# Splitting the narrow last slabs by their own columns, spreading the block sums, and moving the merge sigmoids

## The chip, the cores and the metric

One NeuronCore of a Trainium2 chip runs the whole program. The engines are TensorE (PE; its weight loads are listed as PEld), VectorE (DVE), ScalarE (ACT), GpSimd (POOL) and SyncE (SP), which issues most of the transfers. Time is the device time of one execution in microseconds (us), the median of the runs shown.

## The reference

256 tokens of width 2048 pass through two layers of a first block and one layer of a second block, all in fp32. Cut to what the change touches:

```python
# first block, twice: the input projection, of which the fourth group (rwkv) has 1792 columns
u = rms_norm(h, norm_pre_mix[l])
p = u @ w_in[l]
p_ret, p_hgrn, p_ml, p_rw = split_cols(p, GROUP_COLS)    # 512*3 + 64 + 64 + 128 = 1792 in p_rw
...
# second block: qa, kc, vc, ks, vs, kw, vw and ga are 1024 + 6*256 + 48 columns
proj = h @ w_in
(qa, kc, vc, ks, vs, kw, vw, ga, za, qb, kb, vb, zb, ma, mb) = jnp.split(proj, IN_SPLITS, axis=-1)
...
def compress(t, pe, w1, w2):        # of kc and of vc
    blk = t[:, cidx] + pe[None, None, :, None, :]
    blk = blk.transpose(0, 1, 3, 2, 4).reshape(B, n_c, G, CMP_BLOCK * dh)
    return jax.nn.gelu(blk @ w1) @ w2
...
merged = jax.nn.sigmoid(ma) * ya + jax.nn.sigmoid(mb) * yb     # ma and mb: 2048 columns each
```

## The kernel before

**Products.** Activations lie feature-major: 128 features on the partitions, 256 tokens along the free dimension. A weight is brought in as slabs of four 128-row tiles by 512 columns (1 MB) into a ring of four. Each fp32 product is made from parts: ACT writes a rounded high part of the slab (`high`, L185, tile `w_hi`), DVE subtracts it from the slab to get the low part (`low`, L193, tile `w_lo`), and PE multiplies the high weights with the high and low activations side by side (L214, 512 columns) and the low weights with the high activations (L215, 256 columns). `w_hi` and `w_lo` have two places each. So the high part of slab g+2 waits until PE has used slab g, the low part waits for the high part, and PE waits for the low part.

**A projection.** `Linear` runs over chunks of 512 columns; with an inner size of 2048 a chunk is four slabs. Columns that don't fill a chunk make a last, narrow one: 256 columns in the rwkv projection of each layer (12 full and 4 narrow slabs), 128 columns in the qkv projection of the second block (20 full and 4 narrow slabs). The transfer of a narrow slab brings only its columns, and PE multiplies only those; `high` and `low` run over all 2048 elements of the place (`self.slot`).

**The order on ACT and DVE** comes from `ahead`: for every slab g first the part of slab g+2, then a callback `beside`, and at the last slab of a chunk the epilogue. ACT's epilogue copies the cross sums out of PSUM (L343), waits for DVE's sum (L364, or L366 into `tmp`), and applies a function (L348) if there is one. Most chunks run in a hardware loop of 8 slabs; the last ones of a stage are written out. When the narrow chunk ends, both engines have also split slab 0 of the next stage (`split_next`); the stage ends when all engines are done.

**The block sums.** In the qkv projection `beside` is `Blocks`: DVE adds the position weights to 4 groups of the compressed-key rows, four additions a group (L2871), behind the low parts of slabs 18, 19, 20 and 21, one group each. Before the first group DVE waits for the transfers that gather those rows.

**The merge projection.** `mixes` is the 4096 columns of `ma` and `mb`: 8 chunks of 4 slabs with a sigmoid. On PE all 8 chunks run in a loop of two chunks; on ACT and DVE the first six run in that loop, and the last two are written out. The seven first chunks' sigmoids are in place; the eighth is done in the next stage (`defer`).

Of the kernel before, what the change touches and what calls it, by code (L numbers as in the profile page):

```python
# [6 lines left out]
F32 = mybir.dt.float32  # L7
F32R = mybir.dt.float32r
I32 = mybir.dt.int32
ALU = mybir.AluOpType  # L10
ACT = mybir.ActivationFunctionType
AX = mybir.AxisListType

P = 128
T = 256
D = 2048
# [7 lines left out]
CW = 512  # L24
CB = CW // P
SK = 4
RING = 4
# [6 lines left out]
class Signal:  # L34


    def __init__(self, ctx, nc, name):
        self.sem = ctx.enter_context(nc.semaphore(name))
        self.base = 0
        self.seen = 0  # L40
# [80 lines left out]
class Stream:  # L121
# [56 lines left out]
    def high(self, act, g, i=None):  # L178

        core = self.core  # L180
        if g >= 2:
            self.reached(act, core.slab_used, g - 2, i)
        self.landed(act, g, i)
        at = slice(0, self.slot)
        core.nc.scalar.activation(core.w_hi[:, g % 2, at], core.ring[:, (self.start + g) % RING, at], ACT.Copy)\  # L185
            .then_inc(core.hi_ready, 1)

    def low(self, eng, g, i=None, ops=None):

        core = self.core  # L190
        self.reached(eng, core.hi_ready, g, i)
        at = slice(0, self.slot)
        (ops or core.nc.vector).tensor_tensor(core.w_lo[:, g % 2, at], core.ring[:, (self.start + g) % RING, at],  # L193
                                              core.w_hi[:, g % 2, at].bitcast(F32), ALU.subtract).then_inc(core.lo_ready, 1)

    def used(self, eng, g, i=None):

# [32 lines left out]
class Linear(Stream):  # L230
# [6 lines left out]
    def __init__(self, core, mats, k, col0, cols, dst, kind="copy", func=ACT.Copy, src=None, x0=0, tail=None, row0=0, unrolled=False):  # L237
        self.x0, self.tail, self.row0 = x0, tail, row0
        self.mats, self.dst, self.kind, self.func, self.src_tiles = mats, dst, kind, func, src
        self.kt = k // P  # L240
        self.slabs = self.kt // SK
        self.body = BODY // self.slabs
        self.col0 = col0
        self.m = len(mats)
        full, self.last = divmod(cols, CW)
        self.n_chunks = full * self.m
        assert not (self.m == 2 and self.last)
        self.trips = 0 if unrolled else self.n_chunks // self.body
        self.total = self.n_chunks + (1 if self.last else 0)

        self.ahead_trips = self.trips if self.trips * BODY + 2 <= self.total * self.slabs else self.trips - 1
        super().__init__(core, self.total * self.slabs, BODY)

    def width(self, q):
        return CW if q < self.n_chunks else self.last

    def ends(self, dst, g, i):
        q, s = divmod(g, self.slabs)
        row = self.row0 + s * SK * P
        rows = self.mats[q % self.m][row:row + SK * P, :].rearrange("(k p) n -> p k n", p=P)  # L260
        col = self.col0 + q // self.m * CW
        n = self.width(q)
        dst = dst.rearrange("p (k n) -> p k n", k=SK)[:, :, 0:n]
        if i is None:
            return dst, rows[:, :, col:col + n]
        return dst, rows[:, :, bass.ds(i * (self.body // self.m * CW) + col, n)]

    def ahead(self, eng, part, epilogue, after):

        split = dict(high=self.high, low=self.low)[part]  # L270
        for g in range(self.split, 2):
            split(eng, g)

        assert self.post is None or self.ahead_trips <= 0

        def step(g, i):
            if g + 2 < self.n_slabs:
                split(eng, g + 2, i)
            elif g == self.n_slabs - 2:
                self.split_next(eng, part, after)  # L280
            if self.beside is not None and i is None:
                self.beside(eng, part, self.n_slabs - 1 - g)
            if g % self.slabs == self.slabs - 1:
                q = g // self.slabs
                if self.post is not None and part == "low" and q >= 2:
                    self.post.fold(eng, q - 2)
                if not (self.defer and q == self.total - 1):
                    epilogue(eng, q, i)
                if self.post is not None and part == "high" and q:
                    _, turn, _ = self.where(q - 1, i)  # L290
                    free = self.core.free[(q - 1) % 2]
                    eng.wait_ge(free.sem, free.base + turn + 2)
                    self.post.early_square(eng, q - 1)
                    if q < 3:
                        self.post.scale(eng, q - 1, q)
                    else:
                        last = self.core.free[q % 2]
                        eng.wait_ge(last.sem, last.base + turn + 2)
                        self.post.early_square(eng, q)
                        self.post.load_root(eng)  # L300
            if self.early is not None and i is None:
                self.early(eng, part, self.n_slabs - 1 - g)

        if self.ahead_trips > 0:
            with eng.Fori(0, self.ahead_trips) as i:
                if part == "high" and self.kind == "gate":
                    self.core.nc.scalar.activation(self.core.table[:, :], self.core.const("ones")[:, 0:1], ACT.Silu)
                for g in range(BODY):
                    step(g, i)
        for g in range(max(self.ahead_trips, 0) * BODY, self.n_slabs):  # L310
            step(g, None)
# [17 lines left out]
        eng.wait_ge(free.sem, self.base[free] + q // 2 + 2 + opened)  # L329

    def act_epilogue(self, act, q, i):
        core, nc = self.core, self.core.nc
        par, turn, at = self.where(q, i)
        n = self.width(q) // P
        free, tmp = core.free[par], core.tmp[:, par, 0:n, :]
        trip = 0 if i is None else i * self.body
        self.used(act, (q + 1) * self.slabs - 1, i)

        act.wait_ge(free.sem, self.base[free] + turn + 1)
        if self.kind == "gate" and par == 0:  # L340

            act.wait_ge(core.free[1].sem, self.base[core.free[1]] + turn + 1)
        nc.scalar.activation(tmp, core.ps[:, CB * par:CB * par + n, T:2 * T], ACT.Copy).then_inc(core.cross_copied.sem, 1)  # L343
        if self.plain() or self.kind in ("times", "plus") or (self.kind == "gate" and par == 1):
            return
        act.wait_ge(core.summed.sem, self.base[core.summed] + q + 1 + trip)
        if self.kind == "copy":
            nc.scalar.activation(self.out_tiles(q, at, n), tmp, self.func).then_inc(free.sem, 1)  # L348
        elif self.kind == "mul":
            nc.scalar.activation(tmp, tmp, self.func).then_inc(core.factor_ready.sem, 1)  # L350
        else:
            nc.scalar.activation(tmp, tmp, ACT.Silu).then_inc(free.sem, 1)
# [125 lines left out]
class Idle:  # L478
# [5 lines left out]
    act = pool = sp = pe  # L484
# [233 lines left out]
class Down(Stream):  # L718
# [46 lines left out]
    def __call__(self, eng, part, left):  # L765

        x_split = self.x_high if part == "high" else self.x_low
        if left == 3:
            x_split(eng, 0)
            x_split(eng, 1)  # L770
        elif left == 2:
            x_split(eng, 2)
# [479 lines left out]
class Lead:  # L1252
# [49 lines left out]
    def act(self, act, stream, first_split):  # L1302
# [55 lines left out]
        for q in range(4):  # L1358
            high(q)

    def dve(self, dve, stream, first_split):
# [63 lines left out]
        if first_split == 0:  # L1425
            stream.low(dve, 0)
        norm(1)
        low(0)
        norm(2)
        low(1)  # L1430
# [1394 lines left out]

class Blocks:

    def __init__(self, m, w, qkv):  # L2830
        self.m, self.w, self.qkv = m, w, qkv
# [26 lines left out]

    def __call__(self, eng, part, left):

        if part == "high" or not 4 <= left < 8:
            return
        if left == 7:
            eng.wait_ge(self.moved.rec[0], 16 * 4)
            eng.wait_ge(self.weights.rec[0], 16 * 5)
        g = 7 - left
        for n in range(2):
            view = self.m.arena[:, 52 + 4 * n + g, :].rearrange("p (c b two) -> p b c two", b=8, two=2)
            for half in range(2):
                rows = slice(half * 8, half * 8 + 8)  # L2870
                self.m.nc.vector.tensor_tensor(self.blk[n][:, rows, g * NCMP:(g + 1) * NCMP], view[:, :, half:half + NCMP, 0],  # L2871
                                               self.pe_v[n][:, rows].unsqueeze(2).broadcast_to([P, 8, NCMP]), ALU.add)
# [372 lines left out]
def second_block(m, a, qkv, lead, out_stored, result):  # L3245
# [4 lines left out]
    w_in = a["w_in_2"][0]  # L3250
    ada = m.second("ada")

    def proj(c0, n, dst, kind="copy", func=ACT.Copy, src=None, tail=None):
        return Linear(m, [w_in], D, c0, n, dst, kind, func, src, tail=tail)

    stored, reloaded, fetched = Load(m, "stream_stored"), Load(m, "stream_reloaded"), Load(m, "compress_weights_landed")
    tiles, there, spare = Tiles(m.a(0, N_ARENA)), Tiles(m.h[:, :, :]), Tiles(m.spare[:, :, :])
# [33 lines left out]
    for j in range(8):  # L3291
        g = j // 2
# [10 lines left out]
    add = [masks[:, tt * T:(tt + 1) * T] for tt in range(2)]  # L3303
# [143 lines left out]
```

## Time and profile before

| | us |
|---|---|
| median of 3 runs | 3932.89 |
| lowest and highest | 3929.29, 3940.15 |
| span of the profiled execution | 3928.8 |
| PE busy in it | 3659.1 (93%) |
| DVE, ACT, POOL busy | 2039.1, 1771.8, 1717.0 |

The profiled execution's own time is listed only as its span, which is 0.5 us under the lowest run and 4.1 us under the median. In the timelines below the first number is the start in us from the span's start, the second the duration of the merged group; the bracket at a row's end is how long the engine had been idle and what released it.

### The profile page before, as it was taken

The page shows a single profiled execution, that of the slowest core. Times are in us where ns is not written, and L with a number is a line of the kernel's source. Part 1 is how long each engine was busy: PE and PEld are TensorE (multiplying, and loading weights), DVE is VectorE, ACT ScalarE, POOL GpSimd, SP SyncE. Part 2 cuts the span into 40 slices and gives each one's busy share as a digit, 9 for nine tenths or more (in the row PEclk, how much of TensorE's full clock was granted, in tenths as well). Part 3 has the DMA queues.
Part 4 walks back from the last instruction along what each step waited for, and adds up shares of the span by engine and source line. Part 5 has one row for each costly group of instructions (what it writes and reads, how often), then busy time and mean ns, then how long its engine had stood idle before and what let it go on. Part 6 is the DMA issues. An engine that isn't in the chain of part 4 may idle for free. (4 is left out here: it accounts for less than half of the span.)

```text
span 3928.8 us, 60889 instructions
## 1 busy us (share of the span) xinstructions
PE 3659.1 (93%) x25724; PEld 3246.5 (83%) x25724; DVE 2039.1 (52%) x2013; ACT 1771.8 (45%) x1865; POOL 1717.0 (44%) x824
## 2 busy tenths in 40 slices
PE   8898899899999999798999799999999999989998
PEld 7788888688888887687889688888887788878887
DVE  4747533655555555646542555555556542244474
ACT  4415444544444445415444544444445334544443
POOL 0426566499991000424656399994000045440000
PEclk9999899999999999998999999999999999999999
DMA  5423345477775554423435477775554633426553
GB/s 190 140 66 124 110 139 192 158 240 238 241 241 187 192 182 138 141 67 104 130 118 170 154 246 235 241 241 198 183 186 160 207 105 114 124 89 203 182 174 126
DMA packets 378828, 655.47 MB, mean 167 GB/s; under 512 B 13713, under 2 KB 189921, under 8 KB 377745
## 3 DMA queue, kind: packets, MB, share of 16 engines
q1 hardware_dynamic: 363248, 596.98, 46.8%
q0 software_dynamic: 15392, 55.79, 4.2%
q8 instruction: 142, 2.33, 0.2%
q14 instruction: 46, 0.37, 0.0%
HBM read 645.37 MB, written 6.29 MB: 166 GB/s over the span
## 5 line engine op out<-in xcount | busy, mean ns | idle before, releaser
L214 PE MATMUL ps<-x_parts,w_hi 128*128 128x512 f32 x6160 | 2184.0, 399 | 68.2 <-DVE w_lo L193 25.7
L215 PE MATMUL ps<-x_parts,w_lo 128*128 128x256 f32 x6160 | 1730.8, 281 | 0.0
L193 DVE TENSOR_TENSOR w_lo<-weight_ring,w_hi 128x2048 fp32r<-128x2048 f32 x392 | 957.5, 2443 | 1034.6 <-ACT w_hi L185 1034.4
L214 PEld LDWEIGHTS ps<-x_parts,w_hi 128*128 128x128 f32 x6160 | 1163.8, 189 | 362.3 <-issue 36.9
L185 ACT ACTIVATE w_hi<-weight_ring 128x2048 fp32r<-128x2048 f32 (+1 forms) x412 | 787.9, 1912 | 1153.2 <-PE ps L215 1085.1
L215 PEld LDWEIGHTS ps<-x_parts,w_lo 128*128 128x128 f32 x6160 | 1169.7, 190 | 0.0
L627 PE MATMUL ps<-x_parts,w_hi 128*128 128x256 f32 x2592 | 782.8, 302 | 69.4 <-ACT arena L645 33.7
L628 PE MATMUL ps<-x_parts,w_hi 128*128 128x256 f32 x2592 | 748.0, 289 | 0.0
L629 PE MATMUL ps<-x_parts,w_lo 128*128 128x256 f32 x2592 | 747.0, 288 | 0.0
L627 PEld LDWEIGHTS ps<-x_parts,w_hi 128*128 128x128 f32 x2592 | 512.2, 198 | 101.6 <-issue 58.6
L578 POOL TENSOR_TENSOR w_lo<-weight_ring,w_hi 128x1024 fp32r<-128x1024 f32 (+1 forms) x152 | 376.8, 2479 | 345.9 <-ACT w_hi L575 338.6
L628 PEld LDWEIGHTS ps<-x_parts,w_hi 128*128 128x128 f32 x2592 | 512.9, 198 | 4.5 <-issue 3.6
L629 PEld LDWEIGHTS ps<-x_parts,w_lo 128*128 128x128 f32 x2592 | 511.9, 198 | 0.0
L590 POOL TENSOR_TENSOR w_lo<-weight_ring,w_hi 128x1024 fp32r<-128x1024 f32 (+1 forms) x152 | 354.2, 2330 | 277.3 <-ACT w_hi L587 262.3
L2809 POOL TENSOR_SCALAR spare<-spare,second_vectors 128x512 f32<-128x512 f32 x180 | 406.3, 2264 | 3.9
L2813 POOL TENSOR_TENSOR arena<-arena,spare 128x512 f32<-128x512 f32 x180 | 356.4, 1980 | 14.6
L193 POOL TENSOR_TENSOR w_lo<-weight_ring,w_hi 128x2048 fp32r<-128x2048 f32 (+1 forms) x20 | 91.5, 4577 | 596.3 <-ACT w_hi L185 596.3
L575 ACT ACTIVATE w_hi<-weight_ring 128x1024 fp32r<-128x1024 f32 (+1 forms) x152 | 154.3, 1015 | 276.8 <-PE ps L629 276.8
L587 ACT ACTIVATE w_hi<-weight_ring 128x1024 fp32r<-128x1024 f32 (+1 forms) x152 | 154.3, 1015 | 209.2 <-PE ps L629 196.7
L115 POOL DMA_DIRECT2D spare<-in_w_ada x96 | 73.5, 765 | 150.2 <-POOLq L391 70.8
L115 POOL DMA_DIRECT2D arena<-in_w_ck x4 | 3.3, 826 | 295.2 <-DVE w_lo L193 295.2
L3184 DVE SCALAR_TENSOR_TENSOR arena<-ps,arena 128x256 f32<-128x256 f32 (+1 forms) x40 | 20.4, 553 | 163.8 <-PE ps L3090 129.8
(407 smaller groups left out, 2835.0 us busy)
## 6 DMA issues: line engine op xcount, KB each, us to landing
weight_ring<-in_w_in SPq DMA_DIRECT2D x212, 1024.0 KB, 5.2
weight_ring<-in_w_ffn_gate SPq DMA_DIRECT2D x88, 1024.0 KB, 5.2
weight_ring<-in_w_ffn_up SPq DMA_DIRECT2D x88, 1024.0 KB, 5.2
weight_ring<-in_w_ffn_down SPq DMA_DIRECT2D x88, 1024.0 KB, 5.2
spare<-in_w_ada POOLq DMA_DIRECT2D x96, 512.0 KB, 5.0
weight_ring<-in_w_out SPq DMA_DIRECT2D x32, 768.0 KB, 4.7
weight_ring<-in_w_out SPq DMA_DIRECT2D x24, 1024.0 KB, 5.1
weight_ring<-in_w_br_a SPq DMA_DIRECT2D x8, 1024.0 KB, 5.2
```

Source lines behind the costliest of these rows:

```text
L185: core.nc.scalar.activation(core.w_hi[:, g % 2, at], core.ring[:, (self.start + g) % RING, at], ACT.Copy)\
L193: (ops or core.nc.vector).tensor_tensor(core.w_lo[:, g % 2, at], core.ring[:, (self.start + g) % RING, at], core.w_hi[:, g % 2, at].bitcas ...
L214: mm(out, hi, core.x_parts[:, x, :, :].rearrange("p a t -> p (a t)"), start=first, stop=False)
L215: return mm(out[:, 0:T], lo, core.x_hi[:, x, :], start=False, stop=last)
L575: core.nc.scalar.activation(hi, src, ACT.Copy).then_inc(core.upper_high.sem, 1)
L578: core.nc.gpsimd.tensor_tensor(lo, src, hi.bitcast(F32), ALU.subtract).then_inc(core.upper_low.sem, 1)
L590: core.nc.gpsimd.tensor_tensor(lo, src, hi.bitcast(F32), ALU.subtract).then_inc(core.lo_ready, 1)
L627: mm(out, hi, x_hi, start=(kk == 0), stop=False)
L628: mm(out, hi, x_lo, start=False, stop=False)
L629: last = mm(out, lo, x_hi, start=False, stop=(kk == 2 * self.ks - 1))
L2809: ins = nc.gpsimd.tensor_scalar(to, buf[:, n % 2, k, :], c[:, 2 * s + k:2 * s + k + 1], None, ALU.mult)
L2813: done(pool, nc.gpsimd.tensor_tensor(out, out, buf[:, n % 2, k, :], ALU.add), step)
```

## The change

- `high` and `low` go through a new `filled`: in the narrow slabs they touch only the columns that were loaded (four pieces of 256 or 128 elements), in the others the whole place as before.
- `Blocks` has a table `GROUPS_AT`: group 0 behind the low part of slab 19, groups 1 and 2 behind that of slab 20, group 3 behind that of slab 21.
- `proj`, which builds only the merge projection, sets `unrolled=True`: its chunks are written out on PE, ACT and DVE. With a function and a plain copy it is also `late`: ACT copies the cross sums at the chunk's last slab, and applies the sigmoid one step later, behind the next high part.

```diff
 def high(self, act, g, i=None):
...
-        at = slice(0, self.slot)
-        core.nc.scalar.activation(core.w_hi[:, g % 2, at], core.ring[:, (self.start + g) % RING, at], ACT.Copy)\
+        core.nc.scalar.activation(self.filled(core.w_hi[:, g % 2, :], g), self.filled(core.ring[:, (self.start + g) % RING, :], g), ACT.Copy)\
...
+        lo, src, hi = (self.filled(x, g) for x in (core.w_lo[:, g % 2, :], core.ring[:, (self.start + g) % RING, :], core.w_hi[:, g % 2, :]))
+        (ops or core.nc.vector).tensor_tensor(lo, src, hi.bitcast(F32), ALU.subtract).then_inc(core.lo_ready, 1)
...
+    def filled(self, slab, g):
+
+        n = self.width(g // self.slabs)
+        return slab if n == CW else slab.rearrange("p (k n) -> p k n", k=SK)[:, :, 0:n]
...
+        self.late = unrolled and kind == "copy" and func != ACT.Copy
...
+            if self.late and part == "high" and g % self.slabs == 0 and g:
+                self.act_function(eng, g // self.slabs - 1, None)
...
-                if not (self.defer and q == self.total - 1):
+                if self.late and part == "high" and q < self.total - 1:
+                    self.act_cross(eng, q, None)
+                elif not (self.defer and q == self.total - 1):
                     epilogue(eng, q, i)
...
+    GROUPS_AT = {6: (0,), 5: (1, 2), 4: (3,)}
...
-        return Linear(m, [w_in], D, c0, n, dst, kind, func, src, tail=tail)
+        return Linear(m, [w_in], D, c0, n, dst, kind, func, src, tail=tail, unrolled=True)
```

`act_cross` and `act_function` are the two halves of the former `act_epilogue`, which now calls both.

On DVE, at the end of the qkv projection, from the low part of slab 18 to the stage's end (`w_lo` is a low part, L2871 and L2898 are the block sums, L364 and L387 the chunk sums), before:

```order
L193 TENSOR_TENSOR w_lo<-weight_ring,w_hi 128x2048
L2871 TENSOR_TENSOR arena<-arena 128x8x15 x2
L2871 TENSOR_TENSOR spare<-arena 128x8x15 x2
L193 TENSOR_TENSOR w_lo<-weight_ring,w_hi 128x2048
L2871 TENSOR_TENSOR arena<-arena 128x8x15 x2
L2871 TENSOR_TENSOR spare<-arena 128x8x15 x2
...
L364 TENSOR_TENSOR arena<-ps,tmp 128x1024
L193 TENSOR_TENSOR w_lo<-weight_ring,w_hi 128x2048 x3
L364 TENSOR_TENSOR tmp<-ps,tmp 128x256
```

and of the changed kernel:

```order
L192 TENSOR_TENSOR w_lo<-weight_ring,w_hi 128x2048 x2
L2898 TENSOR_TENSOR arena<-arena 128x8x15 x2
L2898 TENSOR_TENSOR spare<-arena 128x8x15 x2
L192 TENSOR_TENSOR w_lo<-weight_ring,w_hi 128x4x128
...
L192 TENSOR_TENSOR w_lo<-weight_ring,w_hi 128x4x128
L2898 TENSOR_TENSOR arena<-arena 128x8x15 x2
L2898 TENSOR_TENSOR spare<-arena 128x8x15 x2
L387 TENSOR_TENSOR arena<-ps,tmp 128x1024
L192 TENSOR_TENSOR w_lo<-weight_ring,w_hi 128x4x128 x2
L192 TENSOR_TENSOR w_lo<-weight_ring,w_hi 128x2048
L387 TENSOR_TENSOR tmp<-ps,tmp 128x256
```

The two full low parts (slabs 18 and 19) now stand together ahead of the first group, and the low parts of slabs 20 to 23 have a quarter of the elements; the last low part, of the next stage's slab 0, is a full one in both.

On ACT, in the merge projection, one turn of the loop before (`w_hi` is a high part, L343 and L359 the cross copy, L348 and L371 the sigmoid):

```order
L185 ACT_TABLE_LOAD
L185 ACTIVATE w_hi<-weight_ring 128x2048
...
L343 ACTIVATE tmp<-ps 128x1024
L346 ISA
L348 ISA
L348 ACT_TABLE_LOAD
L348 ACTIVATE arena<-tmp 128x1024
...
L343 ACTIVATE tmp<-ps 128x1024
L346 REGISTER_ALU
L348 ISA
L348 ACTIVATE arena<-tmp 128x1024
```

and the first three chunks of the changed kernel:

```order
L184 ACTIVATE w_hi<-weight_ring 128x2048 x5
L359 ACTIVATE tmp<-ps 128x1024
L184 ACTIVATE w_hi<-weight_ring 128x2048
L371 ACT_TABLE_LOAD
L371 ACTIVATE arena<-tmp 128x1024
L184 ACTIVATE w_hi<-weight_ring 128x2048 x3
L359 ACTIVATE tmp<-ps 128x1024
L184 ACTIVATE w_hi<-weight_ring 128x2048
L371 ACTIVATE arena<-tmp 128x1024
```

One high part now stands between each cross copy and its sigmoid, and of two table loads a turn one is left in the whole stage. In the rwkv projections only the shapes change (128x4x256 in place of 128x2048 for slabs 12 to 15), not the order; POOL's and SP's rows are the same in both kernels.

## Rows read from the trace of the kernel before

**Rows 1.** The page, part 1: busy time and share of each engine.

```profile
PE 3659.1 (93%) x25724; PEld 3246.5 (83%) x25724; DVE 2039.1 (52%) x2013; ACT 1771.8 (45%) x1865; POOL 1717.0 (44%) x824
```

**Rows 2.** PE's waits in 75:112, 1500:1660, 2990:3180, 3530:3740: total, times, longest.

```profile
PE ps L214 <- DVE w_lo L193: 3.0, 2, 1.5
...
PE ps L214 <- DVE w_lo L193: 2.8, 3, 1.6
...
PE ps L214 <- DVE w_lo L193: 7.4, 4, 2.9
...
PE ps L214 <- DVE w_lo L193: 6.7, 7, 1.2
```

**Rows 3.** Timeline of the merge projection: ACT, and PE's first wait in the loop.

```profile
3561.63 1.01 ACT L343 ACTIVATE tmp<-ps 128x1024 f32<-128x1024 f32 x1
3565.31 1.28 ACT L348 ACT_TABLE_LOAD   x1 [2.67 <-DVE tmp L366]
...
3567.57 1.90 ACT L185 ACTIVATE w_hi<-weight_ring 128x2048 fp32r<-128x2048 f32 x1
...
3679.59 1.01 ACT L343 ACTIVATE tmp<-ps 128x1024 f32<-128x1024 f32 x1
...
3701.78 1.01 ACT L343 ACTIVATE tmp<-ps 128x1024 f32<-128x1024 f32 x1
...
3571.85 0.50 PE L214 MATMUL ps<-x_parts,w_hi 128*128 128x512 f32 x1 [0.98 <-DVE w_lo L193]
```

**Rows 4.** Timeline at the end of layer 0's rwkv projection: ACT, DVE, PE.

```profile
95.44 1.92 ACT L185 ACTIVATE w_hi<-weight_ring 128x2048 fp32r<-128x2048 f32 x1 [2.20 <-PE ps L215]
...
101.96 2.28 DVE L193 TENSOR_TENSOR w_lo<-weight_ring,w_hi 128x2048 fp32r<-128x2048 f32 x1
...
111.54 0.68 DVE L364 TENSOR_TENSOR arena<-ps,tmp 128x512 f32<-128x512 f32 x1
...
99.74 0.50 PE L214 MATMUL ps<-x_parts,w_hi 128*128 128x512 f32 x1 [1.50 <-DVE w_lo L193]
...
112.55 0.35 PE L627 MATMUL ps<-x_parts,w_hi 128*128 128x256 f32 x1 [2.32 <-PEq L391]
```

**Rows 5.** Tile x_parts, by line: duration in ns, shortest/median/longest.

```profile
L742 ACT ACTIVATE x_parts<-arena x88: 609/612/619, 1216.4 to 2963.3; 128x512 fp32r x64, 128x512 fp32r<-128x512 f32 x24
L750 DVE TENSOR_TENSOR x_parts<-arena,x_parts x88: 682/685/1775, 1218.8 to 2965.7; 128x512 fp32r<-128x512 f32 x88
L1327 ACT ACTIVATE x_parts<-arena x16: 1057/1057/1063, 21.4 to 2228.8; 128x1024 fp32r<-128x1024 f32 x16
L1402 DVE TENSOR_TENSOR x_parts<-arena,x_parts x16: 1216/1220/1226, 24.6 to 2229.9; 128x1024 fp32r<-128x1024 f32 x16
```

**Rows 6.** Timeline at the end of the qkv projection: ACT, DVE, PE.

```profile
3115.32 1.91 ACT L185 ACTIVATE w_hi<-weight_ring 128x2048 fp32r<-128x2048 f32 x1 [3.63 <-PE ps L215]
...
3113.64 0.64 DVE L2871 TENSOR_TENSOR arena<-arena 128x120 f32<-128x120 f32 x2 [5.17 <-DMA arena<-arena]
...
3129.76 1.21 DVE L364 TENSOR_TENSOR arena<-ps,tmp 128x1024 f32<-128x1024 f32 x1
...
3139.09 0.42 DVE L364 TENSOR_TENSOR tmp<-ps,tmp 128x256 f32<-128x256 f32 x1
...
3117.07 0.50 PE L214 MATMUL ps<-x_parts,w_hi 128*128 128x512 f32 x1 [1.79 <-DVE w_lo L193]
3128.83 0.80 PE L214 MATMUL ps<-x_parts,w_hi 128*128 128x512 f32 x1 [2.91 <-DVE w_lo L193]
...
3139.83 0.29 PE L2914 MATMUL ps<-small_consts,tmp 48*128 48x48 f32 x2 [2.06 <-PEq L391]
```

**Rows 7.** Busy times in the window of slab 19: length, PE, PEld, DVE, ACT, POOL, clock, DMA.

```profile
3115.30:3124.50 9.20, 7.43 (x33) 6.45 (x34) 6.08 (x10) 1.91 (x1) 0.00 (x0) 0.81 0.46 133
```

**Rows 8.** Timeline of ACT in the last product (written out): two cross copies.

```profile
3841.74 1.00 ACT L343 ACTIVATE tmp<-ps 128x1024 f32<-128x1024 f32 x1
3864.34 1.00 ACT L343 ACTIVATE tmp<-ps 128x1024 f32<-128x1024 f32 x1
```

More of the change, by code:

```diff
@@ L191, in low @@
         self.reached(eng, core.hi_ready, g, i)
-        at = slice(0, self.slot)
-        (ops or core.nc.vector).tensor_tensor(core.w_lo[:, g % 2, at], core.ring[:, (self.start + g) % RING, at],
-                                              core.w_hi[:, g % 2, at].bitcast(F32), ALU.subtract).then_inc(core.lo_ready, 1)
+        lo, src, hi = (self.filled(x, g) for x in (core.w_lo[:, g % 2, :], core.ring[:, (self.start + g) % RING, :], core.w_hi[:, g % 2, :]))
+        (ops or core.nc.vector).tensor_tensor(lo, src, hi.bitcast(F32), ALU.subtract).then_inc(core.lo_ready, 1)
+    def filled(self, slab, g):
+        return slab[:, 0:self.slot]
     def used(self, eng, g, i=None):
@@ L255, in width, with filled @@
         return CW if q < self.n_chunks else self.last
+    def filled(self, slab, g):
+        n = self.width(g // self.slabs)
+        return slab if n == CW else slab.rearrange("p (k n) -> p k n", k=SK)[:, :, 0:n]
     def ends(self, dst, g, i):
@@ L331, in act_epilogue, with act_cross, act_function @@
     def act_epilogue(self, act, q, i):
+        self.act_cross(act, q, i)
+        self.act_function(act, q, i)
+    def act_cross(self, act, q, i):
+        core, nc = self.core, self.core.nc
+        par, turn, at = self.where(q, i)
+        n = self.width(q) // P
+        free, tmp = core.free[par], core.tmp[:, par, 0:n, :]
+        self.used(act, (q + 1) * self.slabs - 1, i)
+        act.wait_ge(free.sem, self.base[free] + turn + 1)
+        if self.kind == "gate" and par == 0:
+            act.wait_ge(core.free[1].sem, self.base[core.free[1]] + turn + 1)
+        nc.scalar.activation(tmp, core.ps[:, CB * par:CB * par + n, T:2 * T], ACT.Copy).then_inc(core.cross_copied.sem, 1)
+    def act_function(self, act, q, i):
         core, nc = self.core, self.core.nc
@@ L336, in act_epilogue @@
         trip = 0 if i is None else i * self.body
[L337 to L343, printed above, removed]
         if self.plain() or self.kind in ("times", "plus") or (self.kind == "gate" and par == 1):
@@ L2859, in __call__, with add @@
     def __call__(self, eng, part, left):
-        if part == "high" or not 4 <= left < 8:
+        if part == "high" or left not in self.GROUPS_AT:
             return
-        if left == 7:
+        if left == 6:
             eng.wait_ge(self.moved.rec[0], 16 * 4)
             eng.wait_ge(self.weights.rec[0], 16 * 5)
-        g = 7 - left
+        for g in self.GROUPS_AT[left]:
+            self.add(g)
+    def add(self, g):
         for n in range(2):
```

## The prediction

> **What bounds the kernel now.** I read the page's busy times first: PE is busy 93% of the span, twice any other engine's share but for its own weight loads [rows 1]. So an edit can gain only where PE stands still or runs at the lower clock, and the second view is PE's waits, taken for the four stretches that the change touches [rows 2]. There PE waits for DVE's low parts 3.0 and 2.8 us (ends of the two rwkv projections), 7.4 us (end of the qkv projection) and 6.7 us (merge projection). The third view, the timelines, shows why, and more than the waits do: what PE loses around a wait.
>
> In the merge projection seven cross copies mark the chunks. From the first to the sixth, at 3561.63 and 3679.59, five chunks take 117.96 us, or 23.59 each; the next takes 22.19 [rows 3]. The reader is to see the slow ones' chain: the cross copy, 2.67 us of idle ACT until DVE's sum is there, a table load of 1.28, the sigmoid, and only at 3567.57 a high part that PE had released about 2 us before; its low part comes late, and PE waits 0.98 us at 3571.85 [rows 3]. Every second chunk pays the load ahead of the sigmoid, the others at the head of the loop's next turn. The quick chunk has its sigmoid in the same place, but no load.
>
> In narrow slabs PE has half or a quarter of the work and ACT and DVE have all of it. With two places, the chain from a slab's use to the low part of the next but one (1.92 and 2.28 us) must fit behind one slab of PE. In the rwkv projection a narrow slab takes PE 2.80 us (high part released at 95.44, PE waits 1.50 until 99.74) [rows 4]. At the end of qkv it is a quarter of 5.55, 1.4 us.
>
> **Prices.** The trace has no four-piece split of a narrow slab. The nearest rows are splits of activations of the same types and sizes: 1024 elements take ACT 1.06 and DVE 1.22 us, 512 elements 0.61 and 0.69 [rows 5]. Those of 1024 elements write four pieces of 256 with gaps, so I take these values for both widths; from the other side the old 1.92 and 2.28 would be the price if pieces cost as much as the whole, and then the shape edit gains nothing.
>
> **The rwkv ends.** Layer 0, with hardly any waiting: slab 12 starts at 95.44 and ends at 98.24, slab 13 ends at 101.04. On DVE the low part of 13 is done at 97.75 (95.44 + 1.06 + 1.22 and hand-over). Before the low part of 14, small operations and the chunk's sum took 2.28 us (95.44 + 1.92 + 2.28 with hand-over is 99.68; it began at 101.96 [rows 4]); now it begins at 100.03 and ends at 101.25, so PE waits 0.2. Slab 14 ends at 104.1, slab 15 at 106.9. Late next is not PE: the next stage's slab 0 is a full one, its high part runs from 104.1 to 106.05, its low part to 108.35, the tail sum takes 0.68, the stage change 0.33 as before (112.22 to 112.55): the next product starts at 109.4 where it started at 112.55 [rows 4]. Gain 3.15. If the first stages behind it were held by something unmoved, half would stay: 1.5. For layer 1, with 2.8 us of waits in place of 3.0, I take 2.8.
>
> **The qkv end.** Before, DVE stood 5.17 us until 3113.64 for the gather transfer ahead of the first block sums; the low part of slab 19 was queued behind it, and PE waited 1.79 us [rows 6]. Behind that wait the window of slab 19 shows a mean clock of 0.81 over 9.20 us, partly the 1.2 GHz level: 1.75 us more [rows 7]. After: slab 18 ends at 3115.3 as before. The low part of 19 ends at 3114.0 (its high part was released one slab, 5.55, ahead of 3115.32) and the first group follows when the gather has landed: no wait left, with the low part of 20 not needed until 3120.85. Groups 1 and 2, 1.2 us each by the 0.64 of two additions, fit in front of that. Slab 19 ends at 3120.85, slab 20 at 3122.2 (low part of 21 just in time), 21 at 3123.6. Now DVE is late: group 3 (to 3123.4), the chunk's sum of 1.21 (to 3124.6) and the low part of 22 (to 3125.3) make PE wait 1.7. Slabs 22 and 23 end at 3126.75 and 3128.15. The next stage's full slab 0 is again last: high part to 3128.7, low part to 3131.0, tail sum 0.42, stage change 0.32: 3131.75 in place of 3139.83 [rows 6]. Gain 8.1. But PE then stands 3.6 us before the compressed keys' products; behind waits of 1.79 and 2.91 the clock fell in this very stage (the first product behind the second took 0.80 in place of 0.50 [rows 6]), so I charge one more stretch at the lower level, 1.75 by the row above. Net 6.35; bounds 4.6 (two such) and 8.1 (none).
>
> **The merge projection.** Written out, ACT loads the sigmoid's table once, since the plain copies run from it too (the quick chunk shows copies and sigmoids without a load [rows 3]). Behind the next high part even that one load delays nothing: the following high part is due a slab (5.55 us) later, and load and sigmoid take 2.3. What the later sigmoid holds up is only that PSUM half, wanted a whole chunk of 22 us later. So five chunks fall from 23.59 to 22.19: gain 7.0. The Trainium skill, ScalarE: Activation LUTs, section What ACT_TABLE_LOAD costs, has a switch cost 2.66 us in all, a load of 1.28 and a drain of 1.38. By that the five chunks would lose 1.38 more each and the gain would be 13.9; the trace shows the load at 1.28, but chunks of 23.59 leave no room for the drain on PE's path, so the rows decide.
>
> The unrolled stream's own price isn't shown for this stage. The last product is written out, has the same four slabs, and takes 22.60 from cross copy to cross copy [rows 8]. Were its 0.41 the price of being written out, eight chunks would cost 3.3 and leave 3.7. I take nothing: the quick chunk of 22.19 sets the pace on ACT and DVE already written out, and 3.7 is the lower bound. SP's transfers keep their order; the quick chunk ran on them.
>
> **Sum.** 3.15 + 2.8 + 6.35 + 7.0 = 19.3 us, from the profiled span of 3928.8 to 3909.5. The median stands 4.1 us above that span, so 3932.9 goes to 3913.6.
>
> **The rivals.**
> - *Smaller gain, from PE's own pace.* The merge stage falls into the 22.60 pace (3.7), and the qkv end has two lower-clock stretches (4.6): 14.25 in all, 3918.6. For it: both paces are in the trace for equal work. Against it: the merge projection's undisturbed chunk had the quick one. Chance 0.17.
> - *The three projection ends are given back.* The stages behind them start earlier and then wait for an unmoved transfer or chain. Only the merge's 7.0 stays: 3925.9, no change that counts. Against it: the next slabs are loaded when a low part frees the ring, which also moves forward, and those stages start their engines at the same stage change. Nor does the change then do what it says, since narrow splits would only lengthen idle time. Chance 0.12.
> - *Slower: PE starves on the written-out stream.* The merge projection's PE loop of two chunks becomes eight chunks, each instruction run once. It decides from 19.3/8 = 2.4 us a chunk. If each chunk cost two stops as long as the stage change's 2.32 [rows 4], eight would cost 37 and the result be 3951. Against it: the written-out last product would bound the price at 0.41. Chance 0.05.
>
> **How the numbers follow.** My forecast has 0.66, the rivals 0.17, 0.12 and 0.05. A difference of 0.3% (11.8 us) is about what a measurement of this kernel can tell from no change. Forecast and first rival are faster: 0.83; the second is the same: 0.12; the third slower: 0.05. The bounds of the terms give 1.5 + 1.5 + 4.6 + 3.7 = 11.3 to 3.2 + 3.2 + 8.1 + 7.0 = 21.5, or 3911 to 3922; the runs before lie 3.6 below to 7.3 above their median, so I take 3904 to 3924.
>
> **What would show it.** Right: PE's waits for low parts gone from the rwkv ends but for some 0.2 us, one wait near 1.7 at the qkv end behind group 3, a first product after it 8 us nearer to the end of slab 18; cross copies of the merge projection 22.2 apart from first to last, one table load. Wrong: narrow splits at 1.9 and 2.3 us, chunks over 22.6, waits of PE's weight loads for nothing named in the merge stage, or a longer wait at the head of the stages behind the three ends. The size is wrong if the clock falls at other places than before; all later waits move against it.

## The result and the profile after

| | before | after |
|---|---|---|
| median (7 runs each, side by side), us | 3929.81 | 3909.07 |
| lowest to highest | 3922.89 to 3940.15 | 3899.54 to 3916.97 |
| after / before, with its 95% interval | | 0.9945 [0.9933, 0.9958] |
| span of the profiled execution | 3928.8 | 3902.8 |

The change makes the kernel 0.55% faster: 20.7 us, between 16.5 and 26.3 by the interval. The two profiled executions lie 26.0 us apart, and part of that may be chance of the clock. First the spans with the mean granted clock, of the kernel before and of the changed one:

```profile
core 0: 3928.8 us, clock 0.969
```

```profile
core 0: 3902.8 us, clock 0.971
```

The lower of TensorE's two levels (1.2 GHz) is half of the higher, and what the mean clock is short of 1, times the span, is the most that stretches at it can have cost (it counts those in which PE stands, too): 3928.8 × 0.031 = 122 us before, 3902.8 × 0.029 = 113 after. So up to 9 us of the 26 can come from there (the clock is printed to three places, so give or take 4), and only about 3.4 of them lie at a place that the change touches (in before, two stretches of 3.4 us at 1.2 GHz behind PE's waits at the end of the qkv projection, one of them that of [rows 7]). The ends of the stages are therefore compared one by one, each from a fixed instruction to another.

PE's waits after, in 75:112, 1500:1660, 2970:3180 and 3500:3720, around the same stages as [rows 2] (for what, total, times, longest):

```profile
PE ps L650 <- PEq L414: 2.4, 1, 2.4
PE ps L216 <- DVE w_lo L192: 0.2, 1, 0.2
...
PE ps L650 <- PEq L414: 2.4, 1, 2.4
...
PE ps L2941 <- PEq L414: 3.5, 1, 3.5
...
PE ps L216 <- DVE w_lo L192: 1.1, 1, 1.1
...
PE ps L216 <- DVE w_lo L192: 1.9, 2, 1.0
```

The waits for low parts fell from 3.0, 2.8, 7.4 and 6.7 us to 0.2, 0, 1.1 and 1.9. The 1.9 are one wait ahead of the merge projection's second slab and one behind its last chunk; both are in the kernel before as well. The five waits between its chunks there, 4.8 us in all, are gone.

**Ends of the rwkv projections.** Timeline of the changed kernel, layer 0: ACT, DVE, PE; the last row is layer 1's first product behind its end.

```profile
94.94 1.06 ACT L184 ACTIVATE w_hi<-weight_ring 128x1024 fp32r<-128x1024 f32 x1 [3.07 <-PE ps L217]
...
96.03 1.23 DVE L192 TENSOR_TENSOR w_lo<-weight_ring,w_hi 128x1024 fp32r<-128x1024 f32 x1 [4.42 <-ACT w_hi L184]
...
108.04 0.68 DVE L387 TENSOR_TENSOR arena<-ps,tmp 128x512 f32<-128x512 f32 x1
...
100.79 0.50 PE L216 MATMUL ps<-x_parts,w_hi 128*128 128x512 f32 x1 [0.23 <-DVE w_lo L192]
109.04 0.35 PE L650 MATMUL ps<-x_parts,w_hi 128*128 128x256 f32 x1 [2.43 <-PEq L414]
...
1586.67 0.36 PE L650 MATMUL ps<-x_parts,w_hi 128*128 128x256 f32 x1 [2.38 <-PEq L414]
```

From slab 13's high part to the next stage's first product it was 112.55 − 95.44 = 17.11 us [rows 4] and is 109.04 − 94.94 = 14.10. What is left at the end is the full slab 0 of the next stage and the sum, in both kernels.

**End of the qkv projection.** Timeline of the changed kernel: ACT, DVE, PE.

```profile
3106.25 0.63 ACT L184 ACTIVATE w_hi<-weight_ring 128x512 fp32r<-128x512 f32 x1 [3.72 <-PE ps L217]
...
3104.77 0.62 DVE L2898 TENSOR_TENSOR arena<-arena 128x120 f32<-128x120 f32 x2
...
3112.58 0.69 DVE L192 TENSOR_TENSOR w_lo<-weight_ring,w_hi 128x512 fp32r<-128x512 f32 x1 [2.81 <-ACT w_hi L184]
3113.19 0.63 DVE L2898 TENSOR_TENSOR arena<-arena 128x120 f32<-128x120 f32 x2
...
3114.27 1.22 DVE L387 TENSOR_TENSOR arena<-ps,tmp 128x1024 f32<-128x1024 f32 x1
3115.40 1.29 DVE L192 TENSOR_TENSOR w_lo<-weight_ring,w_hi 128x512 fp32r<-128x512 f32 x2
...
3121.99 0.42 DVE L387 TENSOR_TENSOR tmp<-ps,tmp 128x256 f32<-128x256 f32 x1
...
3116.14 0.50 PE L216 MATMUL ps<-x_parts,w_hi 128*128 128x512 f32 x1 [1.14 <-DVE w_lo L192]
3122.74 0.29 PE L2941 MATMUL ps<-small_consts,tmp 48*128 48x48 f32 x2 [3.55 <-PEq L414]
```

The high part at 3106.25 is released by slab 18's end; from there to the next product it is 16.49 us, where it was 3139.83 − 3115.32 = 24.51 [rows 6]. DVE no longer stands before the first group (3104.77): the gather had landed. One wait is left, 1.14 us at 3116.14, behind group 3, the chunk's sum and the low part of slab 22. Then PE stands 3.55 us before the compressed keys' products.

**Merge projection.** Timeline of ACT in the changed kernel:

```profile
3541.17 1.00 ACT L359 ACTIVATE tmp<-ps 128x1024 f32<-128x1024 f32 x1
3545.00 1.93 ACT L184 ACTIVATE w_hi<-weight_ring 128x2048 fp32r<-128x2048 f32 x1 [2.82 <-PE ps L217]
3546.94 1.28 ACT L371 ACT_TABLE_LOAD   x1
3548.24 1.06 ACT L371 ACTIVATE arena<-tmp 128x1024 f32<-128x1024 f32 x1
...
3563.79 1.00 ACT L359 ACTIVATE tmp<-ps 128x1024 f32<-128x1024 f32 x1
...
3676.85 1.00 ACT L359 ACTIVATE tmp<-ps 128x1024 f32<-128x1024 f32 x1
```

One table load, the sigmoid behind the next high part, no wait of PE between the first cross copy and the seventh. But the cross copies lie 22.6 us apart and not 22.2: six chunks take 135.68 us, where they took 3701.78 − 3561.63 = 140.15 [rows 3].

### The profile page after: what moved, and what is told of

The parts are those of the page before. It is cut to its first block and busy times, and to the rows that moved or that the text cites. A ratio compares the mean times of both kernels' runs of the same rounds, so it can differ in the third digit from the quotient of the medians.

```text
span 3902.8 us, 60767 instructions
## 1 busy us (share of the span) xinstructions
PE 3653.5 (94%) x25724; PEld 3241.8 (83%) x25724; DVE 2018.7 (52%) x2013; ACT 1752.7 (45%) x1860; POOL 1715.7 (44%) x824
## 5 line engine op out<-in xcount | busy, mean ns | idle before, releaser
L192 DVE TENSOR_TENSOR w_lo<-weight_ring,w_hi 128x2048 fp32r<-128x2048 f32 (+1 forms) x392 | 936.1, 2388 | 1043.8 <-ACT w_hi L184 1043.8
L184 ACT ACTIVATE w_hi<-weight_ring 128x2048 fp32r<-128x2048 f32 (+3 forms) x412 | 776.2, 1884 | 1180.0 <-PE ps L217 1111.3
L650 PE MATMUL ps<-x_parts,w_hi 128*128 128x256 f32 x2592 | 780.4, 301 | 66.1 <-ACT arena L668 34.3
L650 PEld LDWEIGHTS ps<-x_parts,w_hi 128*128 128x128 f32 x2592 | 509.9, 197 | 98.3 <-issue 54.2
```

What stands on the lines that cost most here:

```text
L184: core.nc.scalar.activation(self.filled(core.w_hi[:, g % 2, :], g), self.filled(core.ring[:, (self.start + g) % RING, :], g), ACT.Copy)\
L192: (ops or core.nc.vector).tensor_tensor(lo, src, hi.bitcast(F32), ALU.subtract).then_inc(core.lo_ready, 1)
L650: mm(out, hi, x_hi, start=(kk == 0), stop=False)
```

## The experiments

Five measures are used for every run. L0, L1: from slab 13's high part in the rwkv projection of layer 0 and of layer 1 to the next stage's first product. qkv: from the end of slab 18 to the next product (the compressed keys' first), and on to the first product of the stage behind those (L627 before, L650 after), which takes in what the clock does on the way. Six chunks: the merge projection's first to seventh cross copy. "Moved sums" stands for `GROUPS_AT`.

| kernel | L0 | L1 | qkv | qkv, on | six chunks |
|---|---|---|---|---|---|
| before | 17.11 | 16.49 | 24.51 | 38.69 | 140.14 |
| changed | 14.10 | 13.65 | 16.49 | 30.66 | 135.68 |
| changed, once more | 14.14 | 13.48 | 16.39 | 32.21 | 135.68 |
| narrow splits alone | 14.14 | 13.49 | 17.50 | 34.50 | 141.15 |
| moved sums alone | 17.14 | 16.48 | 20.83 | 35.00 | 140.54 |
| merge written out and late, alone | 17.14 | 16.44 | 22.94 | 39.85 | 135.68 |
| merge written out, not late | 17.14 | 16.44 | 22.84 | 39.61 | 135.68 |
| changed, PE's merge loop kept | 14.15 | 13.48 | 16.37 | 32.21 | 135.68 |
| merge written out, a load per chunk | 17.13 | 16.43 | 23.93 | 41.13 | 135.68 |
| changed, three groups early | 14.11 | 13.48 | 15.62 | 31.48 | 135.68 |
| before, the table first in each turn | 17.14 | 16.43 | 22.18 | 36.36 | 137.20 |

**1. The narrow splits alone.** Against the changed kernel:

```diff
-    GROUPS_AT = {6: (0,), 5: (1, 2), 4: (3,)}
+    GROUPS_AT = {7: (0,), 6: (1,), 5: (2,), 4: (3,)}
...
-        if left == 6:
+        if left == 7:
...
-        return Linear(m, [w_in], D, c0, n, dst, kind, func, src, tail=tail, unrolled=True)
+        return Linear(m, [w_in], D, c0, n, dst, kind, func, src, tail=tail)
```

> Narrow splits alone; block sums and merge projection as before. Measured locally, from the high part of slab 13 to the next stage's first product (17.1 and 16.5 us before, 14.1 and 13.7 with the whole change): my theory says the same 14.1 and 13.7 here, since nothing else of the change touches those places. At the qkv end, from the high part released by slab 18 to the next stage's first product (24.5 before, 16.5 with the whole change): DVE again stands for the gather ahead of the low part of slab 19, so PE's wait of 1.8 and the clock's fall behind it (another 1.8) stay, and some 20 remain. Total gain about 10 us. Rival, that the narrow splits alone give the whole gain at the qkv end: 16.5 there and a total gain of 14.

Measured: 3915.71 us against 3928.55 (10 and 19 runs), ratio 0.9970 [0.9959, 0.9981]. Both rwkv ends are those of the whole change. The qkv end took 17.50 us, nearer to the rival's 16.5 than to my 20. Timeline of this kernel: DVE before the first group, PE's two waits.

```profile
3100.79 0.63 DVE L2898 TENSOR_TENSOR arena<-arena 128x120 f32<-128x120 f32 x2 [4.13 <-DMA arena<-arena]
...
3104.22 0.50 PE L216 MATMUL ps<-x_parts,w_hi 128*128 128x512 f32 x1 [0.74 <-DVE w_lo L192]
3114.40 0.50 PE L216 MATMUL ps<-x_parts,w_hi 128*128 128x512 f32 x1 [1.15 <-DVE w_lo L192]
```

The gather held DVE until 3100.79, which is 2.7 us ahead of slab 18's end (3103.51), and PE waited 0.74. In the profile of before it was 3113.64 and 3115.32, 1.7 ahead, and the wait 1.79 [rows 6]. How the gather's landing stands to PE differs from execution to execution: in the six profiles with the sums in their old place this first wait is 0.44 to 1.79 us; in the five with the sums moved there is none. Nor did the clock's fall come that I had counted behind it: the granted clock is 1.00 from 3103.5 to 3118.0 in this profile.

**2. The moved sums alone** (one execution). Against the changed kernel, beside the same line of `proj`:

```diff
     def filled(self, slab, g):
 
-        n = self.width(g // self.slabs)
-        return slab if n == CW else slab.rearrange("p (k n) -> p k n", k=SK)[:, :, 0:n]
+        return slab
```

> Block sums spread alone; splits over whole places and merge projection as before. My theory: the rwkv ends stay at 17.1 and 16.5 us; at the qkv end the wait of 1.8 ahead of slab 19 and the clock's fall behind it go, about 3.5 of the 24.5, so 21. Rival, that the moved sums only meet the full low parts of the narrow slabs and push those back: 23 to 24.5. Total gain 3.5 us, less than one look can tell.

Measured: 3928.24 us, the qkv end 20.83. The first wait is gone, three others of 2.94, 1.47 and 1.19 us stay behind the full-size splits. Alone, moving the sums gives 1.4 to 3.7 us against the unchanged ends in the table (22.18 to 24.51); on top of the narrow splits it gives 17.50 − 16.49 = 1.0.

**3. The merge projection's part alone.** `filled` and `GROUPS_AT` as before, `unrolled=True` kept.

> Merge projection alone (written out, sigmoid behind the next high part). From the first to the seventh cross copy: 140.2 us before, 135.7 with the whole change. No wait of PE for low parts between them in either theory. If the slower pace of the chunks (22.6) belongs to the written-out stream, it comes again: 135.7, gain 4.5. If the pace is chance of the run, it can as well be 22.2 a chunk: 133.1, gain 7.

Measured: 3925.79 us against 3928.55 (10 and 19 runs), ratio 0.9992 [0.9981, 1.0003], and six chunks in 135.68. Their gain is 4.5 us, not 7.0; the whole time alone doesn't show it, since the interval takes in 1.

**4. Written out, but the sigmoid in its old place** (one execution). As 3, and:

```diff
-        self.late = unrolled and kind == "copy" and func != ACT.Copy
+        self.late = False
```

> Merge projection written out, but each sigmoid in its old place, right behind its cross copy. If table loads are the cause, one load is left, ahead of the first sigmoid: PE waits once, about 1.0 us, and the six chunks take 134.4 at the quick pace or 136.9 at the slow one; the move of the sigmoids then is worth about 1.2 us in all. Rival, that the sigmoid's place is the cause: waits of about 1 us at every chunk, 140 or more.

Measured: 135.68 again, 3931.33 us in all. Moving the sigmoid behind the next high part is worth nothing. Timeline of ACT in this kernel at the only load:

```profile
3566.42 1.00 ACT L358 ACTIVATE tmp<-ps 128x1024 f32<-128x1024 f32 x1
3567.44 1.28 ACT L370 ACT_TABLE_LOAD   x1
3570.01 1.06 ACT L370 ACTIVATE arena<-tmp 128x1024 f32<-128x1024 f32 x1 [1.28 <-DVE tmp L388]
```

The load begins 0.02 us behind the cross copy, and the sigmoid waits for DVE's sum behind it. In the loop it was the other way round: 2.67 us of idle ACT for the sum, and only then the load, at 3565.31 [rows 3]. In the list of ACT's instructions above, a wait of its own (the ISA row at L348) stands ahead of the load in the loop.

**5. The whole change, with PE's loop of two chunks kept** (one execution; ACT and DVE stay written out):

```diff
+                trips = self.n_chunks // self.body if self.late else self.trips
                 if trips:
                     with pe.Fori(0, trips) as i:
```

> The whole change, but PE keeps its loop of two chunks in the merge projection; ACT and DVE stay written out. If the pace of 22.6 us a chunk belongs to PE's written-out stream, the six chunks between the first and the seventh cross copy take 133.1 us (22.2 each). If it is a pace that PE falls into at the start of a stage, whatever the stream, either 133.1 or 135.7 can come; 135.7 acquits the stream.

Measured: 3905.98 us, six chunks in 135.68. PE's written-out stream isn't what sets 22.6 instead of 22.19.

**6. Written out, with a table load for every sigmoid** (one execution). As 4, and an exponential of one column, into a tile that nothing reads, behind the high part that follows each sigmoid, so that the sigmoid's table is gone each time:

```diff
+            if self.func == ACT.Sigmoid and part == "high" and g % self.slabs == 0 and g:
+                self.core.nc.scalar.activation(self.core.table[:, :], self.core.const("ones")[:, 0:1], ACT.Exp)
             if self.late and part == "high" and g % self.slabs == 0 and g:
```

> Merge projection alone, written out, sigmoids in their old place, and a tiny exponential on one column, whose result nothing uses, behind the first high part of each chunk from the second on: so each sigmoid needs a table load again, as many loads ahead of sigmoids as there are chunks. Theory A, that a load costs by being there: every chunk loses 1 us or more, 142 or more between the first and the seventh cross copy. Theory B, formed on the run with one load: the load goes ahead while ACT waits for DVE's sum, and costs only where the wait stands ahead of it, as in the loop; then no wait of PE, 135.7 (or 133.1 at the quick pace).

Measured: seven loads of the sigmoid's table (and between them those of the exponential's, each with ACT idle for 1.5 us behind it), 135.68 all the same, no wait of PE among the chunks, 3927.83 us in all. Timeline of ACT:

```profile
3564.41 1.00 ACT L360 ACTIVATE tmp<-ps 128x1024 f32<-128x1024 f32 x1
3565.43 1.28 ACT L372 ACT_TABLE_LOAD   x1
3567.99 1.06 ACT L372 ACTIVATE arena<-tmp 128x1024 f32<-128x1024 f32 x1 [1.28 <-DVE tmp L390]
```

The number of loads is not what the loop paid for, which was the reason that my prediction gave.

**7. Group 3 one slab earlier, all else as changed.**

```diff
-    GROUPS_AT = {6: (0,), 5: (1, 2), 4: (3,)}
+    GROUPS_AT = {6: (0,), 5: (1, 2, 3)}
```

> The whole change, with the fourth group of block sums behind the low part of slab 20 too, where DVE had 2.8 us to spare, in place of behind that of 21. If group 3 is what delays the low part of slab 22, PE's last wait at the qkv end (1.1 us) goes, and from slab 18's end to the next stage's first product it takes 15.4 in place of 16.5. Rival, that the chunk's sum alone delays it: a wait of 0.3 to 1 us stays and 16 or more. Total within noise of the whole change.

Measured: the qkv end 15.62 us, 0.8 to 0.9 less than in the three profiles of the change; the wait went from 1.14 to 0.37. Timeline of this kernel, DVE and PE:

```profile
3120.41 1.23 DVE L387 TENSOR_TENSOR arena<-ps,tmp 128x1024 f32<-128x1024 f32 x1 [0.22 <-ACT tmp L359]
3121.55 0.68 DVE L192 TENSOR_TENSOR w_lo<-weight_ring,w_hi 128x512 fp32r<-128x512 f32 x1
...
3122.29 0.50 PE L216 MATMUL ps<-x_parts,w_hi 128*128 128x512 f32 x1 [0.37 <-DVE w_lo L192]
```

So 0.77 of the changed kernel's wait of 1.14 was group 3's; the 0.37 that is left is the chunk's sum ahead of the low part, which was the rival's cause. In all 3908.81 us against 3927.53 (4 and 7 runs), 0.9949 [0.9932, 0.9966]: 0.8 us more can't be told from the change itself.

**8. The changed kernel once more** (one execution), for what repeats.

> The whole change once more, for what differs from run to run. If the pace of 22.6 us in the merge projection is fixed by the code, it comes again; if the full clock behind the 3.6 us of idle PE at the qkv end was chance, this run may show a stretch at 1.2 GHz there, 1.7 to 3.4 us dearer. The lengths of the two rwkv ends should repeat within 0.2 us.

Measured: 3917.97 us, span 3916.2, clock 0.965. The local measures repeat within 0.2 us except the one that takes in the clock: 32.21 for 30.66. Granted clock by windows (length, PE, PEld, DVE, ACT, POOL, clock, DMA) behind the idle PE at the qkv end, of the first profile of the changed kernel and of this one:

```profile
3118.00:3128.00 10.00, 6.45 (x34) 4.12 (x33) 2.63 (x2) 3.55 (x4) 0.00 (x0) 1.00 0.97 307
```

```profile
3130.00:3134.00 4.00, 3.73 (x11) 2.12 (x12) 0.00 (x0) 1.53 (x2) 0.00 (x0) 0.57 1.01 309
```

A mean of 0.57 over 4 us is 3.4 us at 1.2 GHz. The same stretch at 1.2 GHz is in the profiles of 5 and 7, and one of about twice that length in 1 (0.72 over 12 us); only the first profile of the change has none. PE had stood 3.5 us in all of them.

**9. The kernel before, with the sigmoid's table loaded first in each turn** (one execution). To the loop before, which stays a loop, one sigmoid of a column is added, into a tile that nothing reads:

```diff
             with eng.Fori(0, self.ahead_trips) as i:
...
+                if part == "high" and self.func == ACT.Sigmoid:
+                    self.core.nc.scalar.activation(self.core.table[:, :], self.core.const("ones")[:, 0:1], ACT.Sigmoid)
```

> The kernel before, and alone a sigmoid of one column (into a tile that nothing reads) at the head of each turn of the merge projection's loop, so that the sigmoid's table is there before the wait for the sums and no load stands between a chunk's sum and its sigmoid; the load at the head of the turn stays. Theory A (in the loop the wait for the sum is an instruction of its own ahead of the load, so load and sigmoid follow the sum one after the other; inside a turn that costs PE about a microsecond, and the load at the turn's head delays the next high part once more): the transitions inside a turn lose nothing any more (22.2 to 22.6 from cross copy to cross copy), those between turns stay at 23.6 to 24; six chunks from the first cross copy to the seventh 137 to 138.5 instead of 140.1. Theory B (it isn't the load behind the sum; a looped ACT loses the time by its turns and waits as such): 140 as before. The whole time can't tell: 0.1% at most.

Measured: 3932.43 us beside 3932.93; between cross copies 22.19, 23.69, 22.19, 23.91, 22.60 and 22.62 us, six chunks 137.20. Timeline of ACT over one turn, and the only two waits of PE between the chunks:

```profile
3565.32 1.00 ACT L345 ACTIVATE tmp<-ps 128x1024 f32<-128x1024 f32 x1
3569.01 1.06 ACT L350 ACTIVATE arena<-tmp 128x1024 f32 x1 [2.69 <-DVE tmp L368]
...
3587.51 1.00 ACT L345 ACTIVATE tmp<-ps 128x1024 f32<-128x1024 f32 x1
3591.22 1.06 ACT L350 ACTIVATE arena<-tmp 128x1024 f32 x1 [2.71 <-DVE tmp L368]
3592.30 1.28 ACT L309 ACT_TABLE_LOAD   x1
...
3611.20 1.01 ACT L345 ACTIVATE tmp<-ps 128x1024 f32<-128x1024 f32 x1
...
3597.99 0.50 PE L214 MATMUL ps<-x_parts,w_hi 128*128 128x512 f32 x1 [1.24 <-DVE w_lo L193]
...
3643.87 0.50 PE L214 MATMUL ps<-x_parts,w_hi 128*128 128x512 f32 x1 [1.24 <-DVE w_lo L193]
```

Without a load behind the sum, the first chunk of each of the three turns hands over in 22.19, 22.19 and 22.60 us with no wait of PE, though the loop is kept. Where the load at the turn's head still stands between the sigmoid and the next high part, it takes 23.69 and 23.91, with one wait of 1.24 each. So the loop's loss is a load that starts only when the sum is there, with a high part queued behind it: once per chunk, inside the turn by the sigmoid's load, at its end by the one at the head.

## Why the prediction was right, and where its terms were off

The forecast case came in: 3909.07 us for 3913.6, a ratio of 0.9945 where 3913.6 / 3932.9 gives 0.9951. Part of the closeness is luck. The gain of 20.7 us stands beside a forecast of 19.3, but the terms, measured one by one, add up to 16.8 (below): the merge projection gave half of what I had counted, and the other 4 us, within the interval, are in none of my terms. Nor does the range follow from its derivation: 11.3 to 21.5 gives 3911 to 3922, and widened by the runs' 3.6 below and 7.3 above that is 3908 to 3929, not the 3904 to 3924 that I took. The 3909.07 lies under 3911, also because the median of the kernel before came out at 3929.81 this time, 3.1 us under the one that I had started from.

- **Prices of the narrow splits: right.** 1.06 and 1.23 us for 1024 elements, 0.63 and 0.69 for 512, as the splits of activations [rows 5]; four pieces cost 0.02 us extra at most.
- **rwkv ends: right.** 3.0 us for 3.15 and 2.8 for 2.8, with the small wait at the place that the prediction named. The narrow splits alone give all of it (experiment 1).
- **qkv end: right in size, its parts less so.** 16.49 us for 16.43 as predicted, one wait (1.14 for 1.7), of which group 3 makes 0.77 (experiment 7). The 3.5 us idle before the compressed keys' products and the charge of 1.75 for the clock behind it were right in three of five profiles with narrow splits; the first profile of the change had no such stretch, and that of experiment 1 one of twice the length. Taken on to the stage behind, the five unchanged ends are 36.36 to 41.13 us (mean 39.1), the three of the change 30.66 to 32.21 (mean 31.7): 7.4 net, where I had 6.35. What I took too literally was the row of the gather: DVE's 5.17 us and PE's 1.79 [rows 6] are one draw, and unchanged ends go from 22.18 to 24.51. The narrow splits bring most of this gain, the moved sums about 1 on top.
- **Merge projection: the step that failed.** I had five chunks fall from 23.59 to 22.19, 7.0 us, by one load in place of one per chunk, with the sigmoid out of the way. Five fell to 22.61, 4.9 us, and the sixth, which had been a quick one, rose by 0.43: 4.5 over six. Over the whole stage (first product to the next stage's) it is 186.3 to 182.7, 3.6 us: the 3.7 that I held as the lower bound. Both the size and the reason were wrong. The size: I took the quick chunk [rows 3] for the pace of all chunks; they came at the 22.6 of the last product [rows 8], though not because PE's stream is written out (experiment 5). This is the merge half of my first rival. The reason: neither the number of loads (experiment 6) nor the sigmoid's place (experiment 4) matters. What the written-out code changed is that the load no longer waits for the sum. Experiment 9 shows it in the loop itself.
- **The drain.** The Trainium skill, ScalarE: Activation LUTs, section What ACT_TABLE_LOAD costs, has 1.38 us of drain beside a load of 1.28. The trace of the changed kernel confirms the load and has no room for the drain: the high part of 3545.00 ends at 3546.93, the load goes from 3546.94 to 3548.22, the sigmoid starts at 3548.24. The measurement decides. The 13.9 us that I drew from it could not have come in any case: the 23.59 us of a slow chunk are measured, so whatever a load costs is in them already.
- **Given back? Starved?** Neither. The narrow splits alone, which only touch those ends, make the whole kernel faster by 7.5 to 16.1 us (the interval of experiment 1), where nothing would be left if the ends were given back. In the written-out stream PE doesn't wait between the first cross copy and the seventh in any run.

**The sum.** By local measures 3.0 + 2.8 + 7.4 + 3.6 = 16.8 us, within the measured 16.5 to 26.3 but at its lower end. Experiments 1 and 3, timed, give 11.8 and 3.1 by their ratios, and with 1 for the sums about 16. The other 4 us up to 20.7 I can't place. Executions of one kernel differ by more: two profiles of the changed kernel have spans 13.4 us apart (3902.8 and 3916.2) at mean clocks of 0.971 and 0.965. By the working above, these clocks would allow 24 us, so the clock sets a bound and not an account.

**What stays open:** what puts PE into the pace of 22.19 or of 22.6 us a chunk. The traces do show when it changes: in the merge projection of every profile the pace holds from one stop of PE to the next. In the changed kernel PE stops 0.87 us ahead of the second slab, and from there to the stage's end all 495 pairs run at 0.353 us. In the kernel before, the pairs behind the five waits between chunks run at 0.353, 0.347, 0.347, 0.353 and 0.347. In experiment 1, also with the loop, all five run at 0.353, and its six chunks take 141.15 where those of before took 140.14; against it the written-out stream gains 5.5 us instead of 4.5.

## What to carry to other kernels

Where a stage's last slabs are narrow, let every engine's work shrink with them: what fixes the end is the splits' length, and a row of the same size elsewhere in the trace gives the price. Before blaming a table load for a loop's slow turns, look at what it stands behind: here a load that ran during a wait cost nothing, and one that started after the wait put its 1.28 us on ACT's path. Writing the loop out, or loading the table early, moved it. And an undisturbed chunk's time should be checked against undisturbed work elsewhere before it is taken as the pace of all.

## What the runs showed of the hardware

- **Two paces for the same matmuls at the full clock.** A pair (512 and 256 columns) takes 22.19 / 64 = 0.347 us in one chunk and 22.61 / 64 = 0.353 in another. Groups of PE's instructions by line in the quick chunk of before (3679.59 to 3701.78; count, busy, mean ns):

```profile
L214 PE MATMUL ps<-x_parts,w_hi 128*128 128x512 f32 x65 | 22.6, 394 | 0.0
L215 PE MATMUL ps<-x_parts,w_lo 128*128 128x256 f32 x65 | 18.0, 277 | 0.0
```

  and in a chunk of the changed kernel (3586.39 to 3609.01):

```profile
L216 PE MATMUL ps<-x_parts,w_hi 128*128 128x512 f32 x65 | 23.0, 399 | 0.0
L217 PE MATMUL ps<-x_parts,w_lo 128*128 128x256 f32 x65 | 18.3, 281 | 0.0
```

  (Instructions at a window's edge count whole, so the busy time is a little over the window.) The difference is spread over all pairs, with no wait anywhere. From start to start the slow chunk repeats 241, 120, 236, 113, 233, 117 ns to its end, the quick one cycles through 231, 113, 232, 118, 231, 112, 233, 117. In experiment 9 both appear in one loop: 22.19 inside the first two turns, 22.60 inside the third, behind PE's wait at 3643.87.
- **A table load hides in a wait.** Seven loads of 1.28 us cost PE nothing where each began 0.02 us behind the cross copy and ran while ACT waited for DVE's sum (experiment 6).
- **A granted clock that differs between executions of the same code.** Behind the same idle PE of 3.5 us there were no stretch at 1.2 GHz in one profile of the changed kernel and 3.4 us in another (experiment 8).
